# Throw-away matrix products ahead of and between the transpositions of a normalised activation

## The chip, the cores and the metric

The kernel runs on one core of one Trainium2 chip. The metric is the time of one execution on the device in microseconds (us), lower is better; the number quoted for a kernel is the median over its runs.

## The reference, cut to what matters

The program is three residual blocks in a row over one sequence of 256 positions with 1024 channels: two blocks of attention and gated feed-forward, and one of a convolution module and a convolutional feed-forward. Every half block has this form:

```python
mod = (c_act @ ada_w[i] + ada_b[i])[:, None, :]
sh_a, sc_a, g_a, sh_f, sc_f, g_f = jnp.split(mod, 6, axis=-1)
h = rms_norm(x, norm_g[i, 0]) * (1.0 + sc_a) + sh_a
y = moba_attention(h, ...)                       # or diff_attention, swiglu, conformer, conv_ffn
x = x + g_a * rms_norm(y, norm_g[i, 1])
```

`x` is 256 x 1024, all in float32. The change touches only the step from `x` to `h`, where `x` is scaled per position, transposed so that channels lie on the partitions, and then scaled and shifted per channel. It adds products whose results nobody reads.

## The kernel before

There are six stages, s = 0 to 5: attention (0), gated feed-forward (1), differential attention (2), gated feed-forward (3), conformer module (4), convolutional feed-forward (5). Inside a stage TensorE (PE) multiplies weight tiles of 128 x 128 with the activation in 256 columns, and every product is made of three: high part by high part, and the two mixed ones (`col_product`, line 502, its matmul on line 510; `first_pair`, line 516, matmul on line 528, is the same for the first two units of a stage, interleaved by k). ScalarE (ACT) rounds each 128 x 1024 weight unit to its high part (line 968), VectorE (DVE) makes the low part (line 1299), SyncE loads the units.

Each engine has its own stream of instructions written out by hand in the order in which it runs them, and semaphores tie them together. PE never overtakes: what stands first in its stream runs first. At the border between stage s - 1 and stage s its stream is this:

1. the last row products of stage s - 1 into the four banks of `Y` (`row_tile`, line 541),
2. `mod_columns` (line 567, matmul on line 573): 16 products with one moving column each, `acc` against a column of `ones`, which turn the modulation vector into columns in bank 3 of `work`,
3. `pre_norm(s)` (line 603): it waits for `x_ready`, then for the scaled tile t = 0 of `x` (`xs_ready`), makes eight transpositions of 128 x 128 (line 613), then waits for tile 1 and makes eight more,
4. `first_pair(s)` (line 528), 48 products, each k of which waits for its share of `h_lo` (semaphore `hlo`).

A transposition writes `x_bank(s, k)`, columns 0 to 255 of one of the eight PSUM banks. Beside it, the other engines do, in this order: ACT squares `Y` (line 1068), DVE multiplies by the gate and adds into `xt` (lines 1410 and 1414, which signals `x_ready` per tile), ACT squares `xt` (line 979), POOL takes the power -1/2 (line 455), DVE scales tile t into `xs` (line 1342). Once tile 1 of a k is transposed, DVE and ACT scale and shift that bank in place (DVE line 1353, ACT line 1041), ACT rounds to `h_hi` (line 1047) and DVE subtracts to `h_lo` (line 1358); the first product of the stage waits for the first of these.

```python
need(pe, x_ready, 2 * s)
for t in range(TT):
    pe.wait_ge(xs_ready, 2 * s + t + 1)
    for k in range(KT):
        mm = pe.transpose(x_bank(s, k)[:, t * P:(t + 1) * P], xs[:, t, k * P:(k + 1) * P], ident[:])
```

`ones` and `ident` are constant float32 tiles of 128 x 128, made once by POOL at the start.

Of the kernel before, what the change touches and what calls it, by code (L numbers as in the profile page):

```python
# [24 lines left out]
P = 128  # L25
S = 256
D = 1024
H = 8
KT = D // P
# [31 lines left out]
def build(nc, x, c, rel_bias, ada_w, ada_b, norm_g, moba_w_qkv, moba_w_o, diff_w_qkv, diff_w_o,  # L61
# [4 lines left out]
    with ExitStack() as ctx:  # L66
        def sb(name, shape, dt=F32):
            return ctx.enter_context(nc.sbuf_tensor(name, shape, dt))
# [27 lines left out]
        ident = sb("ident", [P, P])  # L96
        ones = sb("ones", [P, P])
# [3 lines left out]
        work = ctx.enter_context(nc.psum_tensor("work", [P, 4, 512], F32))  # L101
# [45 lines left out]
        def x_parts(s, k0, k1):  # L147

            if s == 0 and k0 == 4:
                return Y[:, 2, :].rearrange("p (k n) -> p k n", k=2)  # L150
            banks, at = ((work, 0), (Y, 0), (Y, 2), (work, 2))[k0 // 2]
            at += k0 % 2
            return banks[:, at:at + k1 - k0, 0:S]

        def x_bank(s, k):

            return x_parts(s, k - k % 2, k - k % 2 + 2)[:, k % 2, :]
# [66 lines left out]
        def need(eng, s, v):  # L224

            if not (isinstance(v, int) and v <= 0):
                eng.wait_ge(s, v)
# [273 lines left out]
        def _(pe):  # L501
# [83 lines left out]
            def mod_gate(base, bank, done):  # L585

                mod_gate_half(base, bank, 0)
                mod_gate_half(base, bank, 1).then_inc(done, 1)
# [10 lines left out]
            def mod_gate_f(layer):  # L599
                pe.wait_ge(gemv, 8 * NBLK * (layer + 1))  # L600
                mod_gate(5 * D, GATE_BANK[2 * layer + 1], mod_gf)

            def pre_norm(s):

                if s % 2:
                    pe.wait_ge(mod_ga_used, s // 2 + 1)
                need(pe, x_ready, 2 * s)
                for t in range(TT):
                    pe.wait_ge(xs_ready, 2 * s + t + 1)
                    for k in range(KT):  # L610
                        if s and t == 0 and k == KT - 1:
                            pe.wait_ge(mod_cols_used, s + 1)
                        mm = pe.transpose(x_bank(s, k)[:, t * P:(t + 1) * P], xs[:, t, k * P:(k + 1) * P], ident[:])
                        if t == TT - 1:
                            mm.then_inc(hT, 1)
# [42 lines left out]
            first_sums(0)  # L658
            first_columns(1)
            pre_norm(0)  # L660
            first_sums(1)

# [285 lines left out]
            for s in range(LAST + 1):  # L948
                if s:
                    pre_norm(s)  # L950
                    pe.wait_ge(x_ready, 2 * s)
                else:
                    pe.wait_ge(mod_cols_used, 1)
                if s in (0, 2):
                    attention(s)
                elif s == 4:
                    conformer()
                else:
                    gated(s)
# [917 lines left out]
```

## Time and profile before

| | us |
|---|---|
| median of 3 runs | 1007.51 (1007.48 to 1008.79) |
| the profiled execution, its own time | 1008.37 |
| its span, first to last instruction | 1006.4 |
| PE busy | 968.5 (96%) |
| DVE busy | 822.4 (82%) |
| ACT busy | 543.6 (54%) |
| mean granted clock of TensorE over the span | 0.981 |

Engines are named PE (matmuls), PEld (TensorE's weight loads, which lie beside matmuls), DVE, ACT, POOL and SP. A granted clock of 1.00 is TensorE's full 2.4 GHz and 0.50 is 1.2 GHz. A float32 product is recorded as two matmuls by the profile, a transposition and a product of rounded parts as one. "[1.59 <-DVE xs L1342]" behind a row says that the engine sat idle for 1.59 us before it and what ended that.

### The profile page before, as it was taken

Reading aid. Unit: us, or ns where it says so; the run is one execution under the profiler, and the core shown is the slowest. Engines: PE = TensorE matmul, PEld = TensorE weight load, DVE = VectorE, ACT = ScalarE, POOL = GpSimd, SP = SyncE. Lnnn points to the kernel's source line nnn. Section 1 sums busy time; section 2 is a strip of 40 time slices with the busy share of each in tenths; the row PEclk is TensorE's granted clock in tenths of the full one; section 3 lists DMA queues with packets and bytes.
Section 4 is the critical chain, followed back from the end, with each engine's and each line's share of the span. In section 5 each row is a group of like instructions: output and inputs, shape, how many; then the busy total and the mean of one; then the engine's idle time right before and its main releaser. Section 6 shows DMA issues by size and latency. Waiting matters only on the chain.

```text
span 1006.4 us, 19120 instructions
## 1 busy us (share of the span) xinstructions
PE 968.5 (96%) x6746; PEld 888.1 (88%) x6746; DVE 822.4 (82%) x1215; ACT 543.6 (54%) x1018; POOL 79.7 (8%) x122
## 2 busy tenths in 40 slices
PE   4899999999999999998999999999998999999997
PEld 3899988999999898996999999989996899999996
DVE  4779978788888768777888777789998879987775
ACT  3455545454444467554554444458998455555552
POOL 2100002000000012122300000002320000000000
PEclk9999999999999999998999999989998999999999
DMA  9999973999999865552599999984330549766641
GB/s 345 329 336 340 332 240 101 341 349 330 312 310 311 262 189 166 171 185 67 158 356 348 317 312 307 313 270 127 85 126 0 179 124 298 225 183 186 186 123 42
DMA packets 240655, 233.52 MB, mean 232 GB/s; under 512 B 7513, under 2 KB 208986, under 8 KB 240602
## 3 DMA queue, kind: packets, MB, share of 16 engines
q1 hardware_dynamic: 237824, 226.52, 72.8%
q0 software_dynamic: 1504, 4.80, 1.4%
q10 hardware_dynamic: 1274, 1.52, 0.4%
q8 instruction: 29, 0.48, 0.2%
q14 instruction: 24, 0.20, 0.1%
HBM read 231.75 MB, written 1.06 MB: 231 GB/s over the span
## 4 chain that ended last, share of the span: by engine, by line
PE 51%; DVE 5%; ACT 4%; issue 3%; POOL 1%; DMA 1%; SPq 0%; POOLq 0%; DVEq 0%; ACTq 0%
PE work L510 28%; PE Y L547 13%; PE Y L860 3%; PE work L528 2%; PE work L727 2%; ACT whi L968 1%; DMA raw<-in_ffn_w_in 1%; DVE acc L1309 1%; DVE wlo L1299 1%; DVE mix L1735 1%; ACT whi L1211 1%; ACT wlo L1211 1%; DVE xt L1414 1%; POOL small L482 1%; DVE Y L1410 0%
## 5 line engine op out<-in xcount | busy, mean ns | idle before, releaser
L1299 DVE TENSOR_TENSOR wlo<-raw,whi 128x1024 fp32r<-128x1024 f32 x286 | 346.6, 1221 | 75.6 <-ACT whi L968 75.0
L510 PE MATMUL work<-h_hi,whi 128*128 128x256 f32 x1360 | 382.6, 281 | 2.2 <-DVE h_lo L1358 1.9
L510 PE MATMUL work<-h_hi,wlo 128*128 128x256 f32 x1360 | 380.2, 280 | 0.0
L510 PE MATMUL work<-h_lo,whi 128*128 128x256 f32 x1360 | 380.1, 279 | 0.0
L968 ACT ACTIVATE whi<-raw 128x1024 fp32r<-128x1024 f32 x286 | 297.6, 1054 | 149.7 <-DMA raw<-in_ffn_w_out 42.5
L510 PEld LDWEIGHTS work<-h_hi,whi 128*128 128x128 f32 x1360 | 255.8, 188 | 6.4 <-issue 2.4
L510 PEld LDWEIGHTS work<-h_lo,whi 128*128 128x128 f32 x1360 | 255.3, 188 | 3.1
L510 PEld LDWEIGHTS work<-h_hi,wlo 128*128 128x128 f32 x1360 | 256.2, 188 | 0.0
L1309 DVE SCALAR_TENSOR_TENSOR acc<-ada_raw,csil,acc 128x1024 f32 (+1 forms) x128 | 163.5, 1279 | 6.6 <-DMA ada_raw<-in_ada_w 4.9
L547 PE MATMUL Y<-whi,ab_hi 128*128 128x512 f32 x286 | 90.4, 397 | 0.6 <-DVE ab_lo L1602 0.4
L547 PE MATMUL Y<-whi,ab_lo 128*128 128x512 f32 x286 | 89.8, 395 | 0.0
L547 PE MATMUL Y<-wlo,ab_hi 128*128 128x512 f32 x286 | 89.6, 394 | 0.0
L547 PEld LDWEIGHTS Y<-whi,ab_lo 128*128 128x128 f32 x286 | 53.6, 188 | 12.9
L547 PEld LDWEIGHTS Y<-wlo,ab_hi 128*128 128x128 f32 x286 | 53.6, 187 | 12.9
L426 POOL TENSOR_TENSOR small<-small 128x1 f32<-128x1 f32 x12 | 6.6, 551 | 692.2 <-DVE small L1408 692.2
L547 PEld LDWEIGHTS Y<-whi,ab_hi 128*128 128x128 f32 x286 | 49.1, 188 | 8.7 <-DVE ab_lo L1602 1.1
L1735 DVE SCALAR_TENSOR_TENSOR mix<-mix,taps 128x256 f32<-128x256 f32 x128 | 51.3, 473 | 0.0
L1186 ACT ACTIVATE ab_hi<-mix 128x256 fp32r<-128x256 f32 x66 | 27.0, 410 | 33.9 <-DVE mix L1641 18.0
L1178 ACT ACTIVATE mix<-work 128x256 f32<-128x256 f32 x44 | 16.7, 379 | 47.6 <-PE work L510 47.6
L1211 ACT ACTIVATE wlo<-ident,taps 128x128 fp32r<-128x128 f32 x104 | 40.4, 389 | 0.0
L1211 ACT ACTIVATE whi<-ident,taps 128x128 fp32r<-128x128 f32 x104 | 40.4, 389 | 0.0
L727 PE MATMUL work<-whi,h_hi 128*128 128x256 f32 x128 | 35.9, 281 | 0.9 <-DVE mix L1432 0.7
(213 smaller groups left out, 1335.3 us busy)
## 6 DMA issues: line engine op xcount, KB each, us to landing
ada_raw<-in_ada_w SPq DMA_DIRECT2D x88, 512.0 KB, 6.5
raw<-in_ffn_w_in SPq DMA_DIRECT2D x88, 512.0 KB, 7.8
ada_raw<-in_mod_w SPq DMA_DIRECT2D x48, 512.0 KB, 6.6
raw<-in_ffn_w_out SPq DMA_DIRECT2D x44, 512.0 KB, 5.9
raw<-in_f_up_w SPq DMA_DIRECT2D x44, 512.0 KB, 4.0
raw<-in_moba_w_qkv SPq DMA_DIRECT2D x24, 512.0 KB, 8.1
raw<-in_diff_w_qkv SPq DMA_DIRECT2D x24, 512.0 KB, 8.0
raw<-in_a_pw_w SPq DMA_DIRECT2D x24, 512.0 KB, 5.5
```

What stands on the lines that cost most here:

```text
L510: mm = pe.matmul(dst, w[:, u, ws], h[:, k, :], start=(k == 0 and m == 0), stop=(k == KT - 1 and m == 2))
L528: mm = pe.matmul(work[:, bank, 0:S], w[:, u, ws], h[:, k, :], start=(k == 0 and m == 0), stop=(k == KT - 1 and m == 2))
L547: mm = pe.matmul(Y[:, 2 * t + f, :], a[:, ts], w[:, u, f * 512:(f + 1) * 512], start=(first and m == 0), stop=False)
L727: mm = pe.matmul(work[:, 1, t * S:(t + 1) * S], h[:, k, ts], w[:, 4:6, ws], start=(k == 0 and m == 0), stop=(k == KT - 1 and m == 2))
L860: mm = pe.matmul(Y[:, j, 0:S], diag[w][:, m, :], u[:, j, m:m + S], start=(m == 0 and n == 0), stop=(m == NP - 1 and n == 2))
L968: act.activation(whi[:, u, :], raw[:, u, :], ACT.Copy).then_inc(hi[u], 1)
L1178: act.activation(gate[:, j, :], work[:, 2 * j, 0:S], ACT.Silu).then_inc(gate_done, 1)
L1186: act.activation(a_hi[:, j, :], act32[:, j, :], ACT.Copy).then_inc(ahi, 1)
L1211: d = act.activation(diag[w][:, m, :], ident[:], ACT.Copy, scale=taps[:, j, 36 + w * NP + m:37 + w * NP + m])
L1299: dve.tensor_tensor(wlo[:, u, :], raw[:, u, :], whi[:, u, :].bitcast(F32), ALU.subtract).then_inc(lo[u], 1)
L1309: dve.scalar_tensor_tensor(at, ada_raw[:, q % 4, :], csil[:, ccol:ccol + 1], at, ALU.mult, ALU.add).then_inc(gemv, 1)
L1735: v = dve.scalar_tensor_tensor(sums, u[:, m:m + S], w, sums, ALU.mult, ALU.add)
```

## The change

It adds a helper `keep_busy(bank, n)`: n products of `ones` (stationary) with `ident` (128 moving columns) into columns 256 to 383 of a bank of `work`, where nothing reads them, and which signal nobody. It is called, for stages 1 to 5, ahead of the wait for `x_ready` (6, 3, 6, 2 and 1 products), ahead of the wait for tile 1 in stage 2 alone (3 products), and ahead of the last transposition of tile 1 (2 products in each stage). That is 18 + 3 + 10 = 31 products.

```diff
+            def keep_busy(bank, n):
+
+                for _ in range(n):
+                    pe.matmul(work[:, bank, S:S + P], ones[:], ident[:], start=True, stop=True)
+
             def pre_norm(s):
 
                 if s % 2:
                     pe.wait_ge(mod_ga_used, s // 2 + 1)
+                if s:
+                    keep_busy(2, (6, 3, 6, 2, 1)[s - 1])
                 need(pe, x_ready, 2 * s)
                 for t in range(TT):
+                    if s == 2 and t:
+                        keep_busy(3, 3)
                     pe.wait_ge(xs_ready, 2 * s + t + 1)
                     for k in range(KT):
                         if s and t == 0 and k == KT - 1:
                             pe.wait_ge(mod_cols_used, s + 1)
+                        if s and t and k == KT - 1:
+                            keep_busy(3, 2)
                         mm = pe.transpose(x_bank(s, k)[:, t * P:(t + 1) * P], xs[:, t, k * P:(k + 1) * P], ident[:])
```

PE's stream at the border into stage 1, with the change; the throw-away products are the rows of L606 (output `work`, moving operand `ident`, stationary `ones`), the transpositions those of L624 (L613 before):

```order
714 L573 MATMUL work<-ones,acc 128x1 x16
715 L606 MATMUL work<-ident,ones 128x128 x6
716 L624 MATMUL work<-ident,xs 128x128 x2
717 L624 MATMUL Y<-ident,xs 128x128 x4
718 L624 MATMUL work<-ident,xs 128x128 x4
719 L624 MATMUL Y<-ident,xs 128x128 x4
720 L624 MATMUL work<-ident,xs 128x128
721 L606 MATMUL work<-ident,ones 128x128 x2
722 L624 MATMUL work<-ident,xs 128x128
723 L528 MATMUL work<-h_hi,whi 128x256
```

Six products now stand between the last modulation column and the first transposition, and two in front of the sixteenth transposition; stages 3, 4 and 5 look the same with 6, 2 and 1 in the first place.

The same place at the border into stage 2, where the tiles are also held apart:

```order
1063 L606 MATMUL work<-ident,ones 128x128 x3
1064 L624 MATMUL work<-ident,xs 128x128 x2
1065 L624 MATMUL Y<-ident,xs 128x128 x4
1066 L624 MATMUL work<-ident,xs 128x128 x2
1067 L606 MATMUL work<-ident,ones 128x128 x3
1068 L624 MATMUL work<-ident,xs 128x128 x2
1069 L624 MATMUL Y<-ident,xs 128x128 x4
1070 L624 MATMUL work<-ident,xs 128x128
1071 L606 MATMUL work<-ident,ones 128x128 x2
1072 L624 MATMUL work<-ident,xs 128x128
1073 L528 MATMUL work<-h_hi,whi 128x256
```

Three products went ahead of tile 0, three between the tiles and two in front of the last transposition; no other instruction of any engine moved.

## Rows read from the trace of the kernel before

**Rows 1.** The page, busy time of each engine.
```profile
PE 968.5 (96%) x6746; PEld 888.1 (88%) x6746; DVE 822.4 (82%) x1215; ACT 543.6 (54%) x1018; POOL 79.7 (8%) x122
```

**Rows 2.** Busy time by stretch, with its column heads: inside stage 1.
```profile
core 0: us, PE busy (x) PEld busy (x) DVE busy (x) ACT busy (x) POOL busy (x), PEclk, DMA share, GB/s
...
180.00:340.00 160.00, 159.86 (x1132) 148.94 (x1131) 130.87 (x137) 73.01 (x98) 0.00 (x0) 1.00 1.04 321
```

**Rows 3.** The same view: one stretch before a fall, and the half-clock stretches.
```profile
469.54:472.95 3.41, 3.41 (x31) 3.35 (x30) 3.17 (x6) 1.84 (x4) 1.19 (x3) 1.00 0.01 2
...
152.10:155.51 3.41, 3.38 (x16) 2.85 (x15) 1.82 (x4) 0.72 (x4) 0.55 (x1) 0.50 0.00 0
...
350.07:356.90 6.83, 5.82 (x27) 5.27 (x26) 5.58 (x11) 5.23 (x11) 0.10 (x1) 0.50 0.01 4
...
472.95:479.78 6.83, 5.03 (x22) 4.35 (x22) 5.10 (x12) 3.11 (x7) 0.55 (x1) 0.50 0.00 1
670.93:677.75 6.82, 6.21 (x28) 5.47 (x28) 5.09 (x13) 4.94 (x10) 0.55 (x1) 0.50 0.95 232
773.33:783.57 10.24, 8.22 (x19) 5.49 (x20) 6.79 (x13) 8.06 (x14) 0.73 (x1) 0.50 0.04 8
807.46:810.87 3.41, 3.14 (x15) 2.82 (x15) 1.74 (x6) 0.72 (x3) 0.54 (x1) 0.50 0.55 184
```

**Rows 4.** PE, timeline at the border into stage 1.
```profile
146.75 3.63 PE L573 MATMUL work<-ones,acc 128*128 128x1 f32 x32
151.96 0.54 PE L613 MATMUL work<-ident,xs 128*128 128x128 f32 x2 [1.59 <-DVE xs L1342]
```

**Rows 5.** One line each: two float32 products, and the transpositions (ns min/median/max).
```profile
L933 PE MATMUL work<-ident,small x4: 421/421/581, 776.3 to 777.1; 128*128 128x128 f32 x4
...
L613 PE MATMUL Y<-ident,xs x48: 272/421/421, 27.8 to 810.7; 128*128 128x128 f32 x48
```

**Rows 6.** PE, timeline at the border into stage 2.
```profile
349.17 0.41 PE L613 MATMUL work<-ident,xs 128*128 128x128 f32 x2 [0.68 <-DVE xs L1342]
349.41 0.60 PE L613 MATMUL Y<-ident,xs 128*128 128x128 f32 x4
...
351.02 0.69 PE L613 MATMUL work<-ident,xs 128*128 128x128 f32 x2 [0.77 <-DVE xs L1342]
```

**Rows 7.** DVE, PE and weight load, timeline after the transpositions of stage 1.
```profile
154.40 1.00 DVE L1353 TENSOR_SCALAR work<-work,colA,colB 128x256 f32<-128x256 f32 x2 [0.64 <-PE work L613]
...
156.02 0.35 PE L528 MATMUL work<-h_hi,whi 128*128 128x256 f32 x1 [0.30 <-DVE h_lo L1358]
...
156.71 0.19 PEld L528 LDWEIGHTS work<-h_hi,whi 128*128 128x128 f32 x1 [0.31 <-DVE h_lo L1358]
```

**Rows 8.** Busy time by stretch, instructions of line 528 alone: stages 2 and 4.
```profile
353.20:356.90 3.70, 3.67 (x17) 3.70 (x18) 0.50 0.03 7
356.90:360.00 3.10, 3.10 (x28) 3.10 (x28) 1.00 0.03 7
...
676.10:677.75 1.65, 1.63 (x7) 1.64 (x8) 0.50 0.19 48
```

**Rows 9.** PE, timeline at the border into stage 3.
```profile
469.35 3.63 PE L573 MATMUL work<-ones,acc 128*128 128x1 f32 x32
474.53 0.66 PE L613 MATMUL work<-ident,xs 128*128 128x128 f32 x2 [1.56 <-DVE xs L1342]
...
478.59 0.55 PE L528 MATMUL work<-h_hi,whi 128*128 128x256 f32 x1 [0.24 <-DVE h_lo L1358]
```

**Rows 10.** PE, timeline at the borders into stages 4 and 5.
```profile
667.76 3.93 PE L573 MATMUL work<-ones,acc 128*128 128x1 f32 x32
672.06 0.66 PE L613 MATMUL work<-ident,xs 128*128 128x128 f32 x2 [0.37 <-DVE xs L1342]
...
807.78 0.66 PE L613 MATMUL work<-ident,xs 128*128 128x128 f32 x2 [0.27 <-DVE xs L1342]
```

**Rows 11.** Busy time by stretch, instructions of line 547 alone: inside stage 4.
```profile
779.50:783.57 4.07, 3.99 (x9) 0.50 0.09 18
```

## The prediction

> **What bounds the kernel now.** I read the busy time of the page first: PE is busy for 968.5 of 1006.4 us, DVE for 822.4 [rows 1]. Then busy time by stretch: inside stage 1, from 180 to 340 us, PE works 159.86 of 160.00 us at a granted clock of 1.00 while DVE works 131 and ACT 73 [rows 2]. So in the long loops PE sets the time, and a delay or a gain of PE at a border is carried to the end. What can be won lies at the borders, where PE waits and, in the same place, loses its clock. The same view cut at the changes of the granted clock shows six stretches at 0.50 (1.2 GHz): 3.41, 6.83, 6.83, 6.82, 10.24 and 3.41 us, 37.5 us in all [rows 3]. Five of them lie at the borders into stages 1 to 5, which the change touches. The longest, 773.33 to 783.57, lies inside stage 4, and no product is added there.
>
> What PE did before a fall is in the timeline. From 469.54 to 472.95 PE counts as busy for the whole 3.41 us, and yet the clock falls at 472.95 [rows 3]: what ran there were the modulation columns, which stream one column each (L573, 3.63 us from 469.35) [rows 9]. Into stage 1 they run from 146.75 to 150.38, then PE idles 1.59 us, and the clock falls at 152.10 [rows 3, 4]. The fall is tied to no instruction: it comes 5.35 us after the start of L573 into stage 1 but 3.6 us after it into stage 3 and 3.2 us into stage 4 (146.75, 469.35 and 667.76 against rows 3) [rows 4, 9, 10]. This decides the case. Into stage 1 the new products come before the fall; into stages 3 and 4 the fall comes while L573 still runs, and they come too late to prevent it.
>
> **The price of one product.** No row has it, but L933 is the same form: float32, 128 columns, two products recorded as x4, 421 ns each record at half clock [rows 5]. In a stream only the spacing counts. Four transpositions at full clock take 0.60 us with the last one's 0.27: (0.60 - 0.27) / 3 = 0.11 us per record [rows 5, 6]. At half clock fifteen take 3.14 us, 0.21 each [rows 3]. Two records make a product: **0.22 us at full, 0.42 at half clock**. The 31 products are 6.8 or 13.0 us of PE; the holes hide 1.59, 0.68 + 0.77, 1.56, 0.37 and 0.27 us [rows 4, 6, 9, 10], and PE's wait for the first low part hides something behind the transpositions. The cover is lost when a product takes 0.42 us.
>
> **Stage 1.** Six products are 1.3 us in a hole of 1.59: hidden. The two ahead of the last transposition cost 0.44 at full clock; DVE and ACT work for 1.6 us from 154.40 before the first product can start (156.02), and seven transpositions and two products take 1.2: hidden. If the clock holds, the first transposition of tile 1, for which DVE waited 0.64 us [rows 7], takes 0.27 and not 0.42 us [rows 5]: 0.15 us won. The clock was back at 155.51, before the first product, so no more is to be had. I take -0.15; between 0 and -0.2.
>
> **Stage 2.** Here 17 products ran at half clock in 3.67 us; later 28 took 3.10, 0.11 each [rows 8]. The 17 would take 1.9: 1.8 us. Of this some 0.45 goes back, because at full clock the second k waits for DVE's low part, as it did in stage 1 (0.31 us) [rows 7]. With the 0.15 of the first transposition that makes 1.5. The three products (0.66) fit the hole of 0.68, the next three the hole of 0.77 [rows 6]. If the clock falls nevertheless, three are 1.26 us in each hole, 0.5 late, but PE then has no hole left and should get its clock back sooner. I take -1.3; between -1.5 and +1.0.
>
> **Stage 3.** The fall comes first, so twelve records start at half clock: 2.5 us in 1.56 [rows 9], tile 0 starts 0.95 late. In return PE is busy without a hole from 472.95 and the clock should be back well before 479.78. The products from 478.59 to there ran at half clock: 0.6 us to win, 0.15 at the first transposition, less some 0.5 by which tile 1 starts late. I take -0.25; between -0.75 and +1.5 (0.95 late, plus two products ahead of the last transposition, 0.84, less 0.3 of cover).
>
> **Stages 4 and 5.** Into stage 4 two products at half clock are 0.84 in a hole of 0.37 [rows 10]; seven products at half clock (1.63 us) stood before the clock's return [rows 8], 0.8 to win. I take -0.2; between -0.95 and +1.0. Into stage 5 one product is 0.42 in 0.27 [rows 10], and nothing but transpositions was slow: I take +0.1; between -0.15 and +0.6.
>
> **Inside stage 4** nothing is added, but what is won earlier moves the work against the clock. Nine records of 512 columns took 3.99 us there at half clock [rows 11], 2 us more than they would at full. I take 0, with 1 us either way for the range.
>
> **The sum** is -0.15 - 1.3 - 0.25 - 0.2 + 0.1 = -1.8 us for the profiled execution, whose own time is 1008.37: 1006.6. The median of the runs shown is 1007.51, 0.86 lower. I read this as executions in which less was lost at the borders, so about 0.8 of the 1.8 is not there to be won: 1007.51 - 1.0 = **1006.5 us**.
>
> A rule of the Trainium skill speaks about this. What the row shows: from 807.46 to 810.87 PE ran 15 records, all transpositions, at half clock, and at 810.87 the clock was back, before any product [rows 3]. The page "TensorE: Matmul & The Clock Gate", Part 4 (PE-mode transpose), says that transpositions do not count as activity for the clock in the way that matmuls do. By that rule the new products, 0.2 to 1.3 us ahead of each border, would be all that counts; the clock would fall at every border as before, and the sum would be only the price at half clock, some 2.5 us slower. By that rule, the trace disagrees.
>
> **The rivals.** What a measurement of this kernel can tell from no change is about 0.2%, 2.0 us.
>
> A. *The clock holds at nearly every border*, because the modulation columns count for more than I give them, or because the gain at one border moves the next so that its products come in time. Then -0.2 - 1.5 - 0.75 - 0.95 - 0.15 = -3.5, of which I count 3.0: 1004.5 us. For it: the products fill the holes almost exactly at full clock. Against it: the clock fell at 472.95 with PE nominally busy all through.
>
> B. *Slower: the products run at half clock in front of the transpositions.* The place is the border into stage 3, and stages 1 and 2 where the fall comes as early there; it decides if the clock falls before about 3.6 us after the start of L573, when the products start. Each costs 0.95 (2.5 in 1.56) and 0.5 ahead of the last transposition, and wins back 0.6 because the clock returns sooner: 0.85, in three stages 2.5: 1010.0 us. For it: stages 3 and 4 show just such a fall. Against it: PE without holes leaves half clock earlier.
>
> C. *Transpositions count for nothing*, the rule above, as a mechanism here: no fall is prevented and no stretch shortened, the products cost as in B: 1010.0 us. Against it stands the rise at 810.87.
>
> D. *The change does not do what it says*: the six stretches stay as they are and the products lie in the idle time: 1007.5 us.
>
> **Chances.** My forecast 0.38, A 0.26, B 0.22, C 0.03, D 0.11. The forecast with D reaches from about 1005.6 to 1009. Leaving out a tenth on either side gives the range 1004.4 to 1010.0, which takes in A and nearly all of B. Faster by over 0.2% is A and 0.02 of the forecast: 0.28. Slower by over 0.2% is most of B and C: 0.22. Within: 0.50.
>
> **What would show it.** In the granted clock of the changed kernel: no stretch at 0.50 at the border into stage 1, at most 3.4 us into stage 2 (6.83 before), into stages 3 and 4 shorter than 6.8 us. In the timeline: the new rows at 0.22 us each into stage 1, and at 0.42 into stage 3, where the wait ahead of L613 (1.56 us) is gone. The forecast is wrong if the stretches at the five borders add up to 27 us as before, if they vanish altogether (A), or if DVE's wait for the first transposition of tile 1 grows beyond 0.64 us (B). It would also be wrong if the half-clock time inside stage 4 changes by more than the borders do.

## The result: slower by about 0.2%

| | before | after |
|---|---|---|
| median, 20 runs each | 1006.98 us | 1009.58 us |
| lowest to highest | 1005.44 to 1008.79 | 1005.87 to 1014.53 |
| span of the profiled execution | 1006.4 | 1008.1 |
| mean granted clock in it | 0.981 | 0.976 |

The ratio is 1.0021, 95% interval 1.0013 to 1.0030: 2.1 us slower (1.3 to 3.0). The forecast was 1006.5. (Microseconds beside a ratio are that ratio times the time of before, here and below; the medians themselves differ by 2.6.) Two things stand out beside the median. The runs of the changed kernel spread over 8.7 us, those of before over 3.4. And 1009.89, the profiled run's own time, is an ordinary run of it.

The page's busy time, after:

```profile
PE 975.5 (97%) x6808; PEld 896.7 (89%) x6808; DVE 822.4 (82%) x1215; ACT 544.0 (54%) x1018; POOL 79.9 (8%) x122
```

62 records more than in [rows 1], which are the 31 products, and 7 us more of PE. Busy time by stretch of the changed kernel (columns as in [rows 2]), cut at the changes of the granted clock, in the order stage 1, 2, 3, 4, inside 4, 5 (a stretch from 34.80 to 41.63 in stage 0, where the change adds nothing, is left out):

```profile
150.86:154.27 3.41, 3.35 (x16) 2.79 (x16) 1.73 (x6) 0.73 (x2) 0.55 (x1) 0.50 0.00 0
348.83:352.24 3.41, 3.41 (x18) 3.41 (x17) 1.08 (x4) 2.19 (x4) 0.55 (x1) 0.50 0.16 58
471.71:478.54 6.83, 6.83 (x33) 6.83 (x34) 3.89 (x8) 1.61 (x4) 0.99 (x2) 0.50 0.00 0
673.10:679.92 6.82, 6.16 (x30) 5.79 (x29) 5.46 (x11) 5.22 (x11) 0.21 (x1) 0.50 0.66 162
772.08:785.74 13.66, 12.15 (x32) 8.01 (x31) 10.01 (x18) 11.45 (x20) 0.73 (x1) 0.50 0.09 28
809.63:813.04 3.41, 3.33 (x17) 2.93 (x16) 1.89 (x4) 0.72 (x4) 0.54 (x1) 0.50 0.61 200
```

Against [rows 3]: no fall was prevented. Of the borders only the stretch into stage 2 became shorter, 3.41 us in place of 6.83; the one inside stage 4, to which nothing was added, became longer, 13.66 in place of 10.24. From 471.71 to 478.54 PE is busy for all 6.83 us (5.03 before), so the holes are filled as meant, and the clock is at 0.50 all the same. This is PE's timeline at the border into stage 3 (L606 are the throw-away products, L624 the transpositions, L613 before):

```profile
468.63 4.01 PE L573 MATMUL work<-ones,acc 128*128 128x1 f32 x32
472.51 2.91 PE L606 MATMUL work<-ident,ones 128*128 128x128 f32 x12
475.21 0.63 PE L624 MATMUL work<-ident,xs 128*128 128x128 f32 x2
...
478.19 0.42 PE L624 MATMUL work<-ident,xs 128*128 128x128 f32 x1
478.41 0.67 PE L606 MATMUL work<-ident,ones 128*128 128x128 f32 x4
478.92 0.27 PE L624 MATMUL work<-ident,xs 128*128 128x128 f32 x1
479.07 0.36 PE L528 MATMUL work<-h_hi,whi 128*128 128x256 f32 x1
```

The clock fell 3.1 us after the first modulation column, while the columns still ran. The six products then took 2.7 us (472.51 to 475.21), the first transposition started 6.58 us after the first column in place of 5.18 [rows 9], and the stage's first product 10.44 us after it in place of 9.24.

**Where the 1.7 us of the two profiles lie.** For each border I take the time from the first modulation column (L573) to the start of the last of the 48 products of the first pair (L528). In both timelines these are single rows; the third column is experiment e4 below, in which the clock stays full at every border.

| border into stage | before | after | full clock (e4) |
|---|---|---|---|
| 1 | 15.25 | 15.26 | 15.12 |
| 2 | 15.68 | 15.42 | 14.21 |
| 3 | 15.44 | 16.42 | 15.09 |
| 4 | 14.76 | 15.73 | 14.20 |
| 5 | 13.94 | 13.93 | 13.79 |
| sum | 75.07 | 76.76 | 72.41 |

The borders explain +1.69, the difference of the spans. (Between them parts go up and down: -0.75 ahead of the border into stage 1, +0.72 in stage 1, -0.44 in stage 2, +0.44 in stage 4, none of which the change touches.) The last rows of line 528 at the border into stage 3, before and after, from which such an entry comes:

```profile
L528 PE MATMUL work<-h_hi,wlo x16: 280/280/415, 479.2 to 484.8; 128*128 128x256 f32 x16
```
```profile
L528 PE MATMUL work<-h_hi,wlo x16: 279/279/279, 479.4 to 485.0; 128*128 128x256 f32 x16
```

The table also says how much there was to win at the borders at all: 75.07 - 72.41 = 2.7 us in the profiled execution.

One column of this table is one execution. Experiment e10 below leaves the borders as they were before, and its profile is a second look at them: 15.88, 14.35, 15.76, 14.35 and 13.93 us, 74.27 in all. The same program thus differed by 1.3 us at the border into stage 2, where before had 17 products at half clock and e10 none. A difference in one row can be such a difference of execution; the sum of the changed kernel is above both.

### The profile page after: what moved, and what is told of

The parts are those of the page before. It is cut to its first block and busy times, and to the rows that moved or that the text cites. A ratio compares the mean times of both kernels' runs of the same rounds, so it can differ in the third digit from the quotient of the medians.

```text
span 1008.1 us, 19244 instructions
## 1 busy us (share of the span) xinstructions
PE 975.5 (97%) x6808; PEld 896.7 (89%) x6808; DVE 822.4 (82%) x1215; ACT 544.0 (54%) x1018; POOL 79.9 (8%) x122
```

## The experiments

All were timed beside runs of the kernel before on the same chip; intervals are 95%, and "fall" is the moment at which the granted clock goes from 1.00 to 0.50.

**e1, e2: which of the products costs.** e1 keeps only the 18 ahead of tile 0, e2 only the ten ahead of the last transposition. Both are shown against the changed kernel.

```diff
 # e1
-                    if s == 2 and t:
-                        keep_busy(3, 3)
-                        if s and t and k == KT - 1:
-                            keep_busy(3, 2)
 # e2
-                if s:
-                    keep_busy(2, (6, 3, 6, 2, 1)[s - 1])
-                    if s == 2 and t:
-                        keep_busy(3, 3)
```

> Keeps the 18 products ahead of tile 0 and drops the three between the tiles and the ten ahead of the last transposition. Theory T (the clock falls during the modulation columns, the products ahead of tile 0 then run at half clock and hold up the transpositions): most of the loss stays, 1.3 to 2.5 us slower than before. Theory U (the two products in front of the last transposition stand directly ahead of the stage's first product and are the loss, at either clock): within 0.5 us of before, or faster. Theory V (the loss is that all work is moved against the half-clock stretch inside stage 4): the stretch inside stage 4 differs from before's 10.2 us.

> Keeps only the ten products ahead of the last transposition, two in each of stages 1 to 5. T: at most 5 x 0.3 us, so 0 to 1.5 us slower than before, and less than e1. U: the whole of 2.6 us.

e1: 1007.86 against 1007.39, ratio 1.0009 (1.0000 to 1.0019), so 0.9 us slower (0.0 to 1.9), less than the 1.3 to 2.5 that T expected and at the edge of what can be told from nothing. e2: 1006.34, ratio 0.9995 (0.9986 to 1.0004), no difference to be told. U falls: the two products in front of the last transposition are not the loss. V (all work is moved against the half-clock stretch inside stage 4) falls too: the half-clock stretch inside stage 4 is 13.65 us in e1's profile, as V wants, but it is that long also in the profiles of e2, e5, e6 and e11, none of which can be told from before. In e1's profile the clock fell 3.1 us after the first column into stage 1, as it had into stage 3 of the changed kernel. PE's timeline there:

```profile
145.75 3.96 PE L573 MATMUL work<-ones,acc 128*128 128x1 f32 x32
149.57 2.91 PE L606 MATMUL work<-ident,ones 128*128 128x128 f32 x12
152.28 0.64 PE L620 MATMUL work<-ident,xs 128*128 128x128 f32 x2
...
156.14 0.36 PE L528 MATMUL work<-h_hi,whi 128*128 128x256 f32 x1 [0.28 <-DVE h_lo L1365]
```

The first product comes 10.39 us after the first column, against 9.27 in [rows 4, 7], and the border takes 16.37 in place of 15.25. That is the same delay of 1.1 us as into stage 3 of the changed kernel, at another border and without the two products of the last transposition. In the same kernel the fall into stage 3 came 4.7 us after the first column, when most of the six were done, and the border took 15.24. So in these profiles the price of the six hangs on where the fall happens to be, not on the stage. The three ahead of tile 0 in stage 2 are no better off: there e1's clock fell 2.5 us after the first column, and the first product came 9.70 us after it in place of 8.37.

**e3: what makes the clock fall.** The kernel before, no throw-away product, but the modulation columns move 128 columns of `ones` each. Product m writes columns m to m + 127 of its bank; the next one overwrites all but column m.

```diff
-mm = pe.matmul(mod_bank[s][:, m:m + 1], acc[:, at:at + P], ones[:, 0:1], start=True, stop=True)
+mm = pe.matmul(mod_bank[s][:, m:m + P], acc[:, at:at + P], ones[:], start=True, stop=True)
```

> The kernel before, without any throw-away product; instead each product of the modulation columns (L573) moves 128 columns of ones in place of one, into overlapping columns of the same bank, so that column m keeps its value. Its records are spaced by the weight load (0.11 us) already, which 128 columns at full clock just fill. If T is right in that the one-column products make the clock fall, the five stretches at the borders vanish or nearly so, the run of 32 records stays at 3.5 to 3.8 us, and the kernel is 1.5 to 3 us faster than before. If the clock follows idle time alone, the stretches stay and the time is within 0.5 us of before.

1007.16 against 1007.39, ratio 1.0002 (0.9992 to 1.0012): not faster, so the expectation of 1.5 to 3 us was wrong. But the trace shows what the columns do. In none of the five did the clock fall while the columns ran. The three borders with short holes, into stages 2, 4 and 5, kept the full clock throughout (14.20, 14.21 and 13.79 us); those into stages 1 and 3, with a hole of 1.5 us behind the columns, did not. Busy time by stretch into stage 3, the columns, the hole with tile 0, and what followed:

```profile
467.34:470.90 3.56, 3.56 (x33) 3.54 (x31) 3.31 (x6) 2.03 (x6) 1.38 (x3) 1.00 0.01 2
470.90:474.06 3.16, 1.24 (x10) 0.85 (x8) 2.12 (x5) 1.15 (x2) 0.55 (x1) 1.00 0.00 0
474.06:480.90 6.84, 6.28 (x28) 5.90 (x29) 5.47 (x12) 4.89 (x10) 0.26 (x1) 0.50 0.02 4
```

The fall has moved behind the columns, to the end of a stretch in which PE worked 1.24 of 3.16 us, and so the half clock now lies over the products of the stage: 16.84 us for this border, 1.4 more than before. And widening is nearly free: 32 records take 3.73 us in place of 3.63 (rows of L573 below and in [rows 4]). In the trace of before the weight loads of these columns fill the same time without a gap (3.77 us from 469.11 into stage 3), so the spacing was theirs already.

**e4: wide columns and all products of the change.** The changed kernel with the line above.

> The changed kernel with the wide modulation columns of e3. T: the clock is at full when the throw-away products come, they fit into the holes, and the loss of 2.6 us is gone: as fast as e3 within 0.5 us. U: 2 us or more slower than e3.

1005.45 against 1007.39, ratio 0.9984 (0.9972 to 0.9996): 1.6 us faster than before, where the same products without the wide columns were 2.1 slower. Nothing at a border is at half clock, the mean is 0.994. PE into stage 3:

```profile
467.52 3.73 PE L573 MATMUL work<-ones,acc 128*128 128x128 f32 x32
471.10 1.50 PE L606 MATMUL work<-ident,ones 128*128 128x128 f32 x12
472.72 0.41 PE L624 MATMUL work<-ident,xs 128*128 128x128 f32 x2
...
474.57 0.44 PE L624 MATMUL work<-ident,xs 128*128 128x128 f32 x2 [0.79 <-DVE xs L1353]
...
476.63 0.35 PE L528 MATMUL work<-h_hi,whi 128*128 128x256 f32 x1 [0.52 <-DVE h_lo L1369]
```

The six take 1.6 us and PE still waits 0.52 us for DVE's low part: at full clock the products are hidden, all of them. The first transposition comes 5.20 us after the first column (5.18 before) and the first product 9.11. By itself neither part gains (e3 1.0002, the change 1.0021); both together do.

**e5, e6, e11: taking products out of the change.** e5 keeps only the three between the tiles of stage 2; e6 is the change without the 18 ahead of tile 0; e11 is the change with `(0, 3, 0, 2, 1)` in place of `(6, 3, 6, 2, 1)`.

> Keeps only the three products between the tiles of stage 2. Theory T (products that run at half clock hold up the transpositions): three at half clock are 1.26 us in a hole of 0.77, so at most 0.5 us slower in one border, and within 0.5 us of before in the median. Rival W (the loss is in this place, because tile 1 stands on the path): 1 to 2 us slower than before.

> The changed kernel without the 18 products ahead of tile 0; the three between the tiles and the ten ahead of the last transposition stay. T: the loss of 2.6 us is mostly gone, within 0.8 us of before. If the 18 do not matter, it stays 2 us or more slower.

> The changed kernel without the six products ahead of tile 0 in stages 1 and 3; all others stay (3, 2 and 1 ahead in stages 2, 4, 5, three between, ten ahead of the last transposition). Theory T prices the sixes highest (2.5 us at half clock in a hole of 1.56): two thirds or more of the loss of the changed kernel goes, 0 to 1 us slower than before. If the loss lies in stages 2, 4 and 5, 1.5 us or more slower.

e5: ratio 1.0002 (0.9993 to 1.0012). e6: 1.0000 (0.9991 to 1.0009). e11: 1.0001 (0.9990 to 1.0012), its interval ends below that of the changed kernel (1.0013 to 1.0030). Without the two sixes the loss is gone, so they are needed for it. That they are enough is not shown: no run has them alone, and the other products cost time too where the clock falls early. In e6, without any ahead of tile 0, it fell 3.0 us after the first column into stage 2, and with the three between the tiles and the two at the end the first product came 9.74 us after it in place of 8.37. And e11's profile has no early fall: four come 4.6 to 5.0 us after the first column, and into stage 2 there is none at all. In e6 the clock fell as early as 2.5 us after the first column into stage 1, and this is the same early fall without the six:

```profile
146.54 4.51 PE L573 MATMUL work<-ones,acc 128*128 128x1 f32 x32
151.76 0.66 PE L622 MATMUL work<-ident,xs 128*128 128x128 f32 x2 [0.72 <-DVE xs L1351]
...
155.16 0.96 PE L606 MATMUL work<-ident,ones 128*128 128x128 f32 x4
155.96 0.27 PE L622 MATMUL work<-ident,xs 128*128 128x128 f32 x1
155.99 0.36 PE L528 MATMUL work<-h_hi,whi 128*128 128x256 f32 x1
```

The first product comes 9.45 us after the first column, 0.2 late; with the six it was 1.1 late. The columns themselves stretch (4.51 us in place of 3.63), and it is the hole that takes this up: the first transposition is not late (5.22 us after the first column, 5.21 before).

**e9: the same products ahead of the columns.** e1's 18 products, inside `mod_columns` behind its first wait (against the kernel before).

```diff
+                    if b == b0:
+                        for _ in range((6, 3, 6, 2, 1)[s - 1]):
+                            pe.matmul(work[:, 3, S:S + P], ones[:], ident[:], start=True, stop=True)
                     for n in range(KT):
```

> The 18 products of e1, the same in number and stage, but ahead of the modulation columns (L573) and not behind them; none between the tiles or ahead of the last transposition. Behind the dense row products of the stage before they run at full clock, 1.3 us for six, and move the columns by that much, into the hole. Theory T (the loss comes from products that run at half clock because the clock fell during the columns): no slower than before by more than 0.5 us, and faster than e1. If it is the PE time of the products that costs, wherever they stand: like e1, 0.5 to 1.5 us slower than before.

1008.44 against 1007.37, ratio 1.0010 (1.0000 to 1.0021): as slow as e1, so T's expectation was missed and the other, that PE's time for the products costs wherever they stand, was met. Into stage 1 the products did run at full clock and the stage's first product was not late (9.28 us after the first of them). But the fall came behind the columns. Busy time by stretch, the half clock into stage 1:

```profile
152.80:159.60 6.80, 5.89 (x27) 5.15 (x26) 5.45 (x11) 4.12 (x9) 0.21 (x1) 0.50 0.00 0
```

It begins 6.0 us after the first added product and lasts far into the 48 products: 16.54 us for the border. There are two ways to pay, then. An early fall makes throw-away products hold up the transpositions; a late one lies over the stage's own products. Theory T had only the first. Whether the added products moved the fall to later is not shown: it came 4.7 us after the first column, and the kernels without products have that as well (4.5 in e10). Against the plain cost of PE's time speak e4 and e7, which run 31 and 18 such products and are not slower than before.

**e7: wide columns with the 18 alone** (e4 without the three and the ten).

> Wide modulation columns with the 18 products ahead of tile 0 alone. T: the columns keep the clock up, the 18 fill the hole behind them; the borders into stages 1 and 3 take 15.1 us and those into 2, 4 and 5 take 14.2, 14.2 and 13.8 us from the first column to the last product of the first pair, as in e4, and the time is within 0.5 us of e4's: the other 13 products are not needed.

The borders take 15.12, 14.22, 15.09, 14.22 and 13.80 us, as expected: for them the other 13 are not needed. The time is 1006.70, ratio 0.9992 (0.9983 to 1.0001); that is 1.2 us above e4's median where 0.5 was expected, but the intervals overlap. In e7's profile the half-clock stretch inside stage 4 was 13.7 us, in e4's 10.2.

**e8, e10: the stretch inside stage 4.** e8 is e4, plus wide square sums and 19 products in PE's waits around the layer norm of stage 4, and three in its wait at the start of stage 0. e10 is the kernel before with only the part inside stage 4. The edit also moves two of PE's waits ahead of `mean_sum`.

```diff
+                pe.wait_ge(act_done, fb + KT)
+                pe.wait_ge(gate_done, fb + KT)
+                keep_busy(2, 3)
                 mean_sum(KT - 1, end=True)
...
-mm = pe.matmul(work[:, 2 + t, 0:1], ln_squares[r][:, k, t * P:(t + 1) * P], ones[:, 0:1],
+mm = pe.matmul(work[:, 2 + t, 0:P], ln_squares[r][:, k, t * P:(t + 1) * P], ones[:],
...
                 b2_bank(0)
+                keep_busy(2, 3)
                 b2_bank(1)
-                pe.wait_ge(act_done, fb + KT)
-                pe.wait_ge(gate_done, fb + KT)
...
                 square_sums(0, (0, 1))
+                pe.wait_ge(d_done, 4)
+                busy_y(4)
                 pe.wait_ge(fold_done, 3)
                 square_sums(1, (0,)).then_inc(var_mm, 1)
+                busy_y(4)
...
                 b2_bank(2)
+                keep_busy(2, 5)
```

(`busy_y` is `keep_busy` into columns 256 to 383 of `Y`'s bank 2.)

> e4 with the same treatment inside stage 4: the square sums (L919 of before) move 128 columns of ones in place of one, and 19 throw-away products lie in PE's waits there; three more lie in PE's wait at the start of stage 0. If the half-clock stretch inside stage 4 (10.2 us, nine records of 512 columns at 0.44 us in it) costs what these records say, it vanishes or halves and the kernel is 1 to 2.5 us faster than e4. If DVE and ACT set the time there anyway, within 0.5 us of e4.

> The kernel before with only the part of e8 inside stage 4: wide square sums and 19 products in PE's waits there; the borders as before. If e8's gain over e4 (some 2 us) comes from there, 1 to 2.5 us faster than before; if from the borders, within 0.5 us of before.

e8: 1003.33 against 1007.46, ratio 0.9954 (0.9941 to 0.9968), 4.6 us faster than before (3.2 to 5.9), the lowest median of the study. e10: 1003.95 against 1007.37, ratio 0.9968 (0.9955 to 0.9980), 3.2 us (2.0 to 4.5). With five runs each and overlapping intervals the two can't be told apart; e8's profile still has 3.4 us at half clock inside stage 4. In e10 the stretch at half clock inside stage 4 is gone:

```profile
770.00:783.00 13.00, 12.83 (x72) 9.86 (x71) 9.64 (x18) 11.55 (x20) 0.72 (x1) 1.00 0.13 41
```

and the products behind it start at full clock, as PE's timeline shows:

```profile
774.69 0.71 PE L947 MATMUL work<-ident,small 128*128 128x128 f32 x4 [0.17 <-POOL small L495]
775.33 1.12 PE L909 MATMUL Y<-mix,ones 1*128 1x512 f32 x2
776.38 1.38 PE L606 MATMUL work<-ident,ones 128*128 128x128 f32 x10
777.52 0.71 PE L547 MATMUL Y<-whi,h_hi 128*128 128x512 f32 x2
```

So the place that the change left alone held about as much as all five borders together, for which e4 measured 1.6 us (0.4 to 2.8) and the table 2.7. The gain is above the 2 us that the nine records of [rows 11] name, and its median is above the 2.5 that was the upper end of what was expected of e10. Part of this is that the profile of before had the shorter stretch there: 10.24 us, where the profiles of the changed kernel, e1, e2, e5, e6, e7, e9 and e11, with the same program in stage 4, have 13.65 or 13.66. From the last product of the first pair of stage 4 to the first column into stage 5 it took 121.4 us before, 121.8 to 122.3 in those eight and 118.9 in e10, so 2.5 to 3.5 us less. How much of that is the clock and how much the moved waits, and what the three products in stage 0 add, was not tried by itself.

## Why the prediction was wrong

- **What bounds the kernel, the prices.** Right. A throw-away product takes 0.22 us at full clock (e4: twelve records in 1.50 us, of which the last is some 0.27: 0.11 each) and 0.45 at half clock (2.70 us for six, 472.51 to 475.21), against 0.22 and 0.42 forecast.
- **That the clock falls during the columns into stage 3, and the products come too late.** Right for the changed kernel's profile, and there it decides the border, as rival B said. In part this was luck: in the profiles of e1, e2, e5, e6, e10 and e11 the fall into stage 3 came 4.3 to 5.5 us after the first column, when the columns were done. How often it comes early in the 20 runs of the changed kernel no run shows. That the columns are the reason was only half of it: in e3 they no longer brought the clock down, but behind them, at the two borders with a hole of 1.5 us, it still fell.
- **Stage 1, -0.15.** The clock was not held: it fell 4.9 us after the first column, before the hole ended, and came back before the first product. 0.0 measured.
- **Stage 2, -1.3.** The clock fell here too and returned 3.4 us sooner. 17 products were saved from half clock, but the first came 9.44 us after the first column in place of 8.37, since the throw-away products ran largely at half clock (those between the tiles took 1.43 us, in a hole of 0.77). -0.26 in the table, 1.0 short of the forecast. And the 1.3 was a gain over the one execution that was profiled: e10, whose borders have no added product, also had 3.41 us at half clock here and took 14.35 us, 1.1 less than the changed kernel.
- **Stage 3, -0.25: the step that failed.** I had 0.95 us of delay ahead of tile 0, of which only 0.5 was to reach tile 1, and 0.75 given back. Measured in the profile: tile 0 starts 1.4 us late (the columns, too, took 0.4 longer), the first product 1.2 late, and 0.2 is given back, +0.98. The clock did not come back "well before": the fall came 0.5 us earlier against the columns than before, and the half clock lasted 6.83 us as it had, though PE had no hole (the first 0.8 us of it were still columns). "PE without holes leaves half clock earlier", which I held against rival B, did not hold here.
- **Stage 4, -0.2.** +0.97 measured. The fall came 5.1 us after the first column, not 3.2, and 15 of the stage's products ran at half clock (7 before). Before, into stage 2, the same late fall (5.2 us) had cost 17 products. So this part may be position alone and not the change. In e6, with nothing added ahead of tile 0 here, the fall came as late (5.4 us) and 17 products ran at half clock, 15.86 us for the border: the two products ahead of tile 0 are not needed for it. No run shows it in stage 4 of the kernel before, and the rest stays open.
- **Stage 5, +0.1; inside stage 4, 0.** -0.01 and +0.44 measured, both within their ranges. The half-clock time at the borders went from 27.3 to 23.9 us and that inside stage 4 from 10.2 to 13.7, as much up as down, so less half clock at the borders was no sign of a gain.
- **The sum.** The terms of stages 2, 3 and 4 are 1.0, 1.2 and 1.2 us off in the table, nearly all of the distance from -1.8 to +1.7. The larger fault lies behind the terms: I worked them out for the one position of the fall that the profile showed, and allowed for others only by a discount of 0.8 us on the gain. The profiles of this study show falls from 2.5 to 5.4 us after the first column at one and the same border. For each position there is another sum. A fall 3.1 us after the first column was seen twice at a border with six products, and each time the first product of the stage came 1.1 to 1.2 us late. The chance of 0.22 for B was too small: its mechanism and sign were right, and its size (2.5 us against 2.1) is close, though it was three stages at 0.85 each where one profile shows one such stage at 0.98. Of its stages the two with six products are needed for the loss (e11). What the other 13 products add on top of a late six is not settled: the 18 alone cost 0.9 us (0.0 to 1.9), all 31 cost 2.1 (1.3 to 3.0).
- **Rival A.** It needs a full clock at the columns, which the change does not give. e4 gives it, and is 1.6 us faster where A said 3.0; the table's 2.7 us is what full clock at all borders is worth in one profile.
- **Rival C, the rule on transpositions.** The Trainium skill's page "TensorE: Matmul & The Clock Gate", Part 4, says that transpositions do not count as busy time in the way that other products do. The time of C was that of B, so the median does not tell them apart; the trace does, and it still disagrees: into stage 5 of the changed kernel the clock returned at 813.04, after a stretch from 809.63 in which PE ran transpositions and, in its last 0.2 us, the first of the throw-away products, and no product of the stage.
- **Rival D.** Of the six stretches four kept their length, but the products did not lie in idle time: into stage 3 the hole of 1.56 us is gone and the first product comes 1.2 us late.

## What to carry to other kernels

Before filling a hole to keep TensorE's clock, look at what runs ahead of it: records can fill the timeline and still not hold the clock, as the one-column products did here. Make such products wide first, which cost 0.1 us for 32 records here, where the weight loads set the pace, and fill holes only then. A filler has to be priced at half clock as well, against a hole that also absorbs what half clock does to its neighbours. And a single profile shows a single position of the fall: take several, and put the filler where it does no harm at the worst of them.

## What the runs showed that I had not expected

- **One moving column or 128, the same time.** 32 float32 records of L573 took 3.63 us with one column and 3.73 us with 128. With one column the clock fell while they ran at several borders (into stages 3, 4 and 5 before); with 128 it did so at none of the 20 borders in the profiles of e3, e4, e7 and e8.
- **The position of the fall is not the program's.** Into stage 1 it came 5.4 us after the first column (before), 2.5 (e6), 5.0 (e11) and 4.5 (e10), with the same instructions ahead of it at this border in all four; with six products behind the columns it came at 4.9 (after) and 3.1 (e1).
- **A kernel can get slower at a higher clock.** The mean granted clock has a median of 0.981 over the 20 runs of the changed kernel and of 0.978 over 27 runs of before (those timed with e8). The run of 1011.61 us had 0.984. The loss goes with PE's time for instructions whose results nobody reads, at the wrong moment, and not with a lower mean. The mean has a blind spot: it reads as full what lies ahead of the first change of the clock that was recorded (39.46 us in before), though transpositions took 0.42 us there, as at half clock.
- **More spread.** 8.7 us from lowest to highest in place of 3.4. That this comes from the position of the fall fits the profiles; the other runs have no trace that would show it. In the other series before spread over 3.4 to 4.2 us, e1 over 4.7 and e11 over 6.4.
